# The recurrence's preparation of the first 256 tokens beside the projection's last 15 tiles

## The reference

```python
h = rms_norm(x, norm_w[l], 1e-6)
proj = h @ w_in[l]                        # 1024 -> 4224 columns, 33 blocks of 128
cols, gate, q, k, v, diff_gate = split(proj)   # cols: r | k | v | decay in | rate in
shifted = concat([prev_row, cols[:-1]])
r, k, v, xw, xa = split(cols + (shifted - cols) * shift_mu)
w = -softplus(-(decay_w0 + tanh(xw) @ decay_lora_b)) - 0.5
decay, a = exp(-exp(w)), sigmoid(iclr_a0 + xa @ iclr_lora_b)
kk = l2_normalised_per_head(k * key_k);  k = k * (1 + (a - 1) * key_a)
# per head, token after token:
S = S * decay + (S @ -kk) (kk * a)^T + v k^T;   y = S @ r
```

## Time and profile before

| what | value |
|---|---|
| median of 3 runs | 4490.38 us |
| the profiled execution's own time | 4491.03 us |
| its span, first to last instruction | 4489.1 us |
| mean granted TensorE clock | 0.949 |
| busy: PE, DVE, ACT, POOL | 4002.1, 2066.5, 1726.1, 519.2 us |
| projection matmuls, three lines together | 929.9 + 934.4 + 918.1 us |

### The profile page before, as it was taken

One profiled execution on the slowest core, in us unless ns is written; L12 is line 12 of the kernel. 1 busy time (PEld: TensorE's weight loads), 2 busy tenths in 40 slices (PEclk: granted clock), 3 DMA queues, 4 the chain that ended last, 5 costly groups with the idle time before them and its releaser, 6 DMA issues.

```text
span 4489.1 us, 113506 instructions
## 1 busy us (share of the span) xinstructions
PE 4002.1 (89%) x49138; PEld 3486.6 (78%) x49138; DVE 2066.5 (46%) x4539; ACT 1726.1 (38%) x3547; POOL 519.2 (12%) x273
## 2 busy tenths in 40 slices
PE   7999999699978888879899999988999698988798
PEld 7999999588865565558899999976888555655588
DVE  6111111678845555554331111117887455565465
ACT  3000000677755665552200000006777465665421
POOL 5222221000000000011032222200000000000111
PEclk9999999799998999989999999988999898998899
DMA  3111111211114354344211111111111242543532
GB/s 139 72 71 72 68 67 52 69 42 50 45 52 138 124 177 140 92 148 163 98 71 72 69 70 71 72 63 43 46 51 35 82 156 85 174 137 93 172 136 83
DMA packets 224389, 410.46 MB, mean 91 GB/s; under 512 B 32402, under 2 KB 132756, under 8 KB 210068
## 3 DMA queue, kind: packets, MB, share of 16 engines
q1 hardware_dynamic: 208916, 313.75, 22.2%
q10 hardware_dynamic: 14976, 89.46, 5.0%
HBM read 296.39 MB, written 106.76 MB: 90 GB/s over the span
## 4 chain that ended last, share of the span: by engine, by line
PE 68%; DVE 11%; ACT 10%; issue 5%; PEld 3%; DMA 2%; SPq 2%; POOL 0%; ACTq 0%; DVEq 0%; PEldq 0%
PE psum L2148 11%; PE psum L2145 11%; PE psum L2147 11%; PE psum L1374 4%; PE psum L1402 4%; PE psum L717 2%; PE psum L1390 2%; ACT arena L1178 2%; PE psum L1138 2%; PE psum L1708 2%; PE psum L1709 2%; PE psum L1710 2%; PE psum L788 1%; DVE arena L1294 1%; PE psum L1130 1%
## 5 line engine op out<-in xcount | busy, mean ns | idle before, releaser
L2145 PE MATMUL psum<-x_hi,w_parts 128*128 128x416 f32 x2640 | 929.9, 352 | 44.3 <-POOL w_parts L2066 18.4
L2148 PE MATMUL psum<-x_hi,w_parts 128*128 128x416 f32 x2640 | 934.4, 354 | 0.0
L2147 PE MATMUL psum<-x_lo,w_parts 128*128 128x416 f32 x2624 | 918.1, 350 | 0.0
L2078 DVE TENSOR_TENSOR arena<-psum,arena 128x416 f32<-128x416 f32 x330 | 195.2, 593 | 1240.4 <-PE psum L2148 1236.5
L334 ACT ACTIVATE arena<-arena 128x256 f32<-128x256 f32 x16 | 8.0, 501 | 1479.2 <-DVE arena L462 1479.2
L2145 PEld LDWEIGHTS psum<-x_hi,w_parts 128*128 128x128 f32 x2640 | 497.7, 189 | 51.4 <-POOL w_parts L2066 20.9
L2147 PEld LDWEIGHTS psum<-x_lo,w_parts 128*128 128x128 f32 x2624 | 494.5, 188 | 8.9 <-issue 0.6
L2148 PEld LDWEIGHTS psum<-x_hi,w_parts 128*128 128x128 f32 x2640 | 497.1, 188 | 3.1
L1281 DVE TENSOR_SCALAR_CACHE_REDUCE arena<-psum 128x512 f32<-128x512 f32 (+3 forms) x640 | 357.7, 608 | 295.3 <-PE psum L1374 158.7
L1402 PE MATMUL psum<-arena 128*128 128x128 f32 x2176 | 310.7, 285 | 64.0 <-ACT arena L1187 46.8
L1374 PE MATMUL psum<-arena 64*128 64x512 f32 (+3 forms) x1280 | 324.3, 610 | 39.7 <-DVE arena L1281 21.7
(11 more groups left out here) (348 smaller groups left out, 6650.5 us busy)
## 6 DMA issues: line engine op xcount, KB each, us to landing
out_proj_t<-arena ACTq DMA_DIRECT2D x66, 1040.5 KB, 4.2
arena<-in_cache_k SPq DMA_DIRECT2D x256, 256.0 KB, 2.9
arena<-in_cache_v SPq DMA_DIRECT2D x256, 256.0 KB, 3.0
arena<-in_w_in SPq DMA_DIRECT2D x66, 512.0 KB, 3.5
arena<-out_proj_t SPq DMA_DIRECT2D x96, 257.0 KB, 3.3
arena<-out_proj_t SPq DMA_DIRECT2D x24, 1024.0 KB, 5.9
x_res<-in_x SPq DMA_DIRECT2D x10, 1664.0 KB, 13.2
m_raw<-mixed_t SPq DMA_DIRECT2D x8, 1664.0 KB, 10.9
```

The costliest lines, as they stand in the source:

```text
L2078: dve.tensor_tensor(ost[:, b % 2, 1 + g * TG:1 + (g + 1) * TG], bank[q % banks_of(l)][:, 0:TG], RSTD[:, cols(g)], ALU.mult).then_inc(p_ev, 1)
L2145: pe.matmul(bank[q % n][:, 0:TG], w_hi[:, b % 3, k, :], x_hi[:, g, k, :], start=(k == 0), stop=False)
L2147: pe.matmul(bank[q % n][:, 0:TG], w_hi[:, b % 3, k, :], xl, start=False, stop=False)
L2148: mm = pe.matmul(bank[q % n][:, 0:TG], w_lo[:, b % 3, k, :], x_hi[:, g, k, :], start=False, stop=(k == KT - 1))
```

## The change

- The last three blocks are taken group by group rather than block by block. The order of the 15 tiles is (30,0), (31,0), (30,1), (32,0), (31,1), (32,1), then (30,2), (31,2), (32,2) and so on. `LEAD_TILE` is the index of the first.
- These 15 tiles are stored one by one by SyncE, each right after its eviction; blocks 0 to 29 are stored as before by ScalarE. Block 32's evictions wait for the stores of block 30's tiles in the same `ost` buffer. The end of the phase waits for the stores on SyncE.
- Slots -4 to -2 of the recurrence are issued in the projection: ScalarE's as `rwkv_scalar(act, LEAD)` behind its last store, VectorE's between evictions, TensorE's ten steps at the tile's start or half (`LEAD_STEPS`), SyncE's loads between the tile stores. The recurrence itself runs from slot -1, with the raw rows of m = 2 loaded in the projection too.
- Six constants are loaded behind the weights, the three masks after tile 5. VectorE waits for six (L457 waited for nine), and for the masks only in the recurrence.
- GpSimd's memset of a column of E moves to the end of its projection program.
- Bank 3 is kept for the preparation: both layers' tiles use seven banks, 0 to 2 and 4 to 7; layer 0's sums of squares go to bank 3 rather than 7.
- The recurrence's arrays are placed anew in SBUF. Those that the first 256 tokens need lie in x_lo's first two groups; `raw`, the copies and other working arrays of m = 0 and 1 in x_hi's first two groups and the raw weight buffers, so they may be written when the tiles of these groups (and the last weight split) are done.
- Semaphores that both phases use are no longer shared with other phases.

```diff
-        SLOTS = range(-4, NU + 3)
+        LEAD, SLOTS = range(-4, -1), range(-1, NU + 3)
...
+        def load_raw(sp, l, m):
+            if m:
+                pV.wait(sp, m - 1, sV_XV)
+            for j in (1, 0, 2):
+                in_raw.inc(sp.dma_start(raw[:, j, :, :], rows(l, j * RW + m % 2 * 2 * P, 2 * P, 2, m // 2 * TQ, TQ + 1)))
+            in_raw.close()
...
             for s in SLOTS:
                 u, t, n, q, r, m, lt = roles(s)
                 if lt is not None:
...
+                    load_lora(sp, l, lt)
+                if m is not None and m > 2:
+                    load_raw(sp, l, m)
...
-            for s in SLOTS:
+            for s in slots:
                 u, t, n, q, r, m, lt = roles(s)
                 if m is not None:
                     mixes(m)
+                if m == 0:
+                    act.wait_ge(p_mm, LEAD_TILE + 6)
+                    act.wait_ge(p_ws, CB + 1)
...
-        SEQ_P = [(b, g) for g in range(NG) for b in range(2)] + [(b, g) for b in range(2, CB) for g in range(NG)]
+        SEQ_P = [(b, g) for g in range(NG) for b in range(2)] + [(b, g) for b in range(2, CB - 3) for g in range(NG)]
+        LEAD_TILE = len(SEQ_P)
+        SEQ_P += [(CB - 3 + i, g) for i, g in ((0, 0), (1, 0), (0, 1), (2, 0), (1, 1), (2, 1))] + [(b, g) for g in range(2, NG) for b in range(CB - 3, CB)]
+        LEAD_STEPS = {(5, 1): (0, sT_ZW), (6, 1): (0, sT_ZA), (7, 1): (0, sT_SS), (8, 1): (0, sT_RN), (9, 0): (0, sT_BO),
+                      (10, 0): (1, sT_ZW), (10, 1): (1, sT_ZA), (11, 1): (1, sT_SS), (12, 0): (1, sT_RN), (13, 0): (1, sT_BO)}
...
-        banks_of = lambda l: 8 if l else 7
+        PB = (0, 1, 2, 4, 5, 6, 7)
...
         def proj_sync(sp, l):
...
+            lead_consts(sp, l)
+            sp.wait_ge(p_st[0], stores(l, 0) + 16 * 7)
+            sp.wait_ge(p_st[1], stores(l, 1) + 16 * 7)
+            load_lora(sp, l, 0)
+            for i, (b, g) in enumerate(SEQ_P[LEAD_TILE:]):
+                sp.wait_ge(p_ev, LEAD_TILE + i + 1)
+                c = slice(0 if g == 0 else 1 + g * TG, 1 + (g + 1) * TG)
+                sp.dma_start(PT[bass.ds(l * COLS + b * P, P), c], ost[:, b % 2, c]).then_inc(p_st[b % 2], 16)
+                if i == 3:
+                    load_raw(sp, l, 0)
+                if i == 5:
+                    lead_masks(sp)
+                if i == 7:
+                    load_raw(sp, l, 1)
+                    load_lora(sp, l, 1)
+                if i == 11:
+                    load_raw(sp, l, 2)
+            for u in range(2):
+                sp.wait_ge(p_st[u], stores(l + 1, u))
...
-            for b in range(CB):
+            for b in range(CB - 3):
                 act.wait_ge(p_ev, LAST[b] + 1)
                 act.dma_start(PT[bass.ds(l * COLS + b * P, P), :], ost[:, b % 2, :]).then_inc(p_st[b % 2], 16)
-            for u in range(2):
-                act.wait_ge(p_st[u], stores(l + 1, u))
+            rwkv_scalar(act, LEAD)
...
-            for q in range(2 * NG, len(SEQ_P)):
+            for q in range(2 * NG, LEAD_TILE):
                 evict(q)
+            lead_vector(dve)
+            for i in range(6):
+                evict(LEAD_TILE + i)
+            for m in range(2):
+                if m:
+                    prep_vector(dve, 0, sV_BV)
+                    pV.close()
+                else:
+                    dve.wait_ge(p_ws, CB + 1)
+                mixed_vector(dve, m, sV_XK)
+                mixed_vector(dve, m, sV_XR)
+                mixed_vector(dve, m, sV_XV)
+                if m:
+                    evict(LEAD_TILE + 9)
+                prep_vector(dve, m, sV_LD)
+                prep_vector(dve, m, sV_SCAN)
+                evict(LEAD_TILE + (10 if m else 6))
+                for k in (sV_KF, sV_RKB, sV_MX, sV_RC, sV_R, sV_K):
+                    prep_vector(dve, m, k)
+                if m:
+                    lora_vector(dve, 1)
+                evict(LEAD_TILE + (11 if m else 7))
+                for k in (sV_KKN, sV_A, sV_BB, sV_B):
+                    prep_vector(dve, m, k)
+                evict(LEAD_TILE + (12 if m else 8))
+            for i in (13, 14):
+                evict(LEAD_TILE + i)
...
                 for k in range(KT):
                     if q == 0 and k == 4:
                         pe.wait_ge(p_ws, 2)
+                    if k % 4 == 0 and (q - LEAD_TILE, k // 4) in LEAD_STEPS:
+                        m, step = LEAD_STEPS[q - LEAD_TILE, k // 4]
+                        if step == sT_ZW and m == 0:
+                            pe.wait_ge(r_cst, 16 * 6)
+                        prep_tensor(pe, m, step)
+                        if step == sT_BO:
+                            pT.close()
```

More of the change, by code:

```diff
@@ L2 @@
 import math
+from collections import namedtuple
 from contextlib import ExitStack
@@ L214, in build @@
         phase_sems()
[L215 to L218, removed]
+        x_group = KT * TG
+        x_hi_at = KT * TOK
+        RA0 = cv(4, 2, TQ)
+        Bf0, Kf0, Vf0, bv0 = [cv(4, TQ) for _ in range(4)]
+        mX1, mL, eye2 = cv(CH), cv(len(LEVELS), CH), cv(CH)
+        assert cv.at <= 2 * x_group
+        cv.at = 2 * x_group
+        RA1, RA2 = cv(4, 2, TQ), cv(4, 2, TQ)
+        Bf1, Kf1, Vf1, bv1, bv2 = [cv(4, TQ) for _ in range(5)]
+        Z = cv(3, 4, CH)
+        assert cv.at <= x_hi_at
+        cv.at = x_hi_at
+        raw = cv(3, 2, TQ + 1)
+        after_raw = cv.at
+        cop_first = cv(3, 2, TQ)
+        assert cv.at <= x_hi_at + x_group
+        cv.at = x_hi_at + x_group
+        xk_first, xr_first, tw_first, ta_first, L_first, kf_first = [cv(2, TQ) for _ in range(6)]
+        assert cv.at <= x_hi_at + 2 * x_group
+        cv.at = 2 * KT * TOK + 6 * KT * P
+        kkn_first, rkb_first, Ei_first = [cv(2, TQ) for _ in range(3)]
+        assert cv.at <= 2 * KT * TOK + 8 * KT * P
+        cv.at = after_raw
         BS, SK = cv(3, 8, 3, CH), cv(3, 8, 2, CH)
@@ L451, in rwkv_scalar, with mixed_vector @@
                     lora_tanh(lt)
-        def rwkv_gpsimd(pool, l):
-            pool.memset(E[:, :, :, 0:1], 1.0).then_inc(r_once, 1)
-        def rwkv_vector(dve, l):
-            dve.wait_ge(r_cst, 16 * 9)
-            dve.memset(Z[:, :, :, :], 0.0)
+        def mixed_vector(dve, m, k):
+            j, dst = {sV_XK: (1, prep_of(m).xk), sV_XR: (0, prep_of(m).xr), sV_XV: (2, Vf[m // 2 % 2][:, m % 2 * 2:m % 2 * 2 + 2, :])}[k]
+            pA.wait(dve, m, {sV_XK: sA_CK, sV_XR: sA_CR, sV_XV: sA_CV}[k])
+            for c in range(2):
+                i_ = dve.scalar_tensor_tensor(dst[:, c, :], raw[:, j, c, 0:TQ], prm[:, m % 2 * 2 + c, j:j + 1], prep_of(m).cop[:, j, c, :], ALU.mult, ALU.add)
+            pV.inc(i_)
@@ L515, in lora, with rwkv_vector @@
[L515 to L520 removed]
+            lora_vector(dve, 0)
+        def rwkv_vector(dve, l):
+            dve.wait_ge(r_msk, 16 * 3)
+            dve.memset(Z[:, :, :, :], 0.0)
             def masked(u, v):
@@ L2069, in proj_gpsimd @@
                         low(pool, g, p_lp, True)
+            pool.memset(E[:, :, :, 0:1], 1.0).then_inc(r_once, 1)
         def proj_vector(dve, l):
@@ L2073, in evict @@
                 b, g = SEQ_P[q]
-                if b >= 2:
+                if b == CB - 1:
+                    sent = sum(x[0] % 2 == b % 2 for x in SEQ_P[LEAD_TILE:q])
+                    dve.wait_ge(p_st[b % 2], stores(l, b % 2) + 16 * ((CB - 3) // 2 + sent))
+                elif b >= 2:
                     dve.wait_ge(p_st[b % 2], stores(l, b % 2) + 16 * (b // 2))
```

314 lines of the change are left out of this document (159 added, 155 removed).

## The result

The changed kernel took 4417.9 us (median of 4 runs, 4411.85 to 4421.63), the kernel before 4490.91 (4 runs, 4482.67 to 4492.69). The ratio is 0.9842 [0.9823, 0.9862]: faster by 73 us, where 64 were forecast. The profiled execution took 4421.63, its span is 4419.8.

What follows compares the result with a forecast made beforehand. TensorE alone bounds the last 15 tiles, then 48.5 us a layer lie on the path; after the change 11.5 + 3.5 + 1.5 = 16.5. Gain 64.0 for two layers: 4491.0 - 64.0 = 4427.0 us, own range 4414 to 4438.

Steps and rivals of the forecast that it cites:

- Term 1: TensorE's ten preparation steps inside the last 15 projection tiles, paid in full: 11.5 us a layer, ends 10.5 and 14.
- The waits: In the 15 tiles every TensorE step has its input in time: 0 us, four steps with 1.2 to 1.5 to spare.
- Term 2: From the last store's issue to the first scores: 3.5 us with the smaller store, ends 3.3 and 5.2.
- Term 3: Slot -1 starts at a slow granted clock: +1.5 us a layer, ends +3 and -3.6.
- rival D: Over the hand-over the clock never falls, since 4.3 us idle is close to 3.5: 4417 us; chance 0.05.
- A: Steps in the 15 tiles wait some 1.5 us at four margins: 4439 us, up to 4450 with clock falls; chance 0.16.
- B: Waits in the 15 tiles let the clock fall and it stays down: slower, 4560 us; chance 0.04.
- C: Something else holds the recurrence's start, half or less of 32 us a layer gained: 4459 to 4490; chance 0.05.
- much over 19 us: Sign of being wrong: slot -1, the recurrence's first slot behind the barrier, lasting much longer than 19 us.
- Other stages changed by more than 2 us: Sign of being wrong: attention or output projection, outside the changed stretch, differing by more than 2 us.
- L723 5 to 6 us behind the last projection matmul: Expected profile sign at the hand-over: first scores starts 5 to 6 us after the last projection matmul, some 32 us earlier.

Runs made afterwards that it cites:

- warm_slot_again: Changed kernel plus 12 unread projection matmuls over the hand-over and 19 small ones in slot -1; 4424.84 us, against 4427.26 for the changed kernel beside it.

## Why the prediction was right

**What bounds it.** TensorE alone set the 15 tiles, and all between the last store and `scores` was on the path: the profile after bears out both, since the tiles grew by TensorE's own steps alone (79.13 of 79.13 us busy) while VectorE took on 24.5 us and ScalarE 22.8 at no cost.

**Term 1, the ten steps:** 11.5 forecast, 11.13 measured in each layer. The 1.23 us that the warm weight loads gave for the four-instruction steps already held the change between two kinds of matmul; the doubling showed the mean step to be 0.86 of matmuls and 0.26 paid once. The upper end of 14 added 0.25 a step for this a second time. That the 0.26 is this change is a reading and not isolated by a run.

**The waits:** none forecast, none seen. The clock that the prediction set up tile by tile, against layer 0 of the profile after (0 at 715.27; "ready" is the end of the instruction that makes the input):

| step | stands, forecast | stands | ready, forecast | ready | margin |
|---|---|---|---|---|---|
| ZA, m = 0 | 30.6 | 30.7 | 29.2 | 29.4 | 1.3 |
| SS, m = 0 | 36.2 | 36.4 | 33.5 | 33.5 | 2.9 |
| RN, m = 0 | 41.9 | 41.9 | near 38 | 38.0 | 3.9 |
| BO, m = 0 | 45.2 | 45.3 | 44.0 | 44.0 | 1.4 |
| ZA, m = 1 | 54.2 | 54.4 | 52.9 | 52.9 | 1.5 |
| SS, m = 1 | 59.8 | 60.1 | 57.0 | 57.2 | 2.9 |
| RN, m = 1 | 63.1 | 63.4 | 61.6 | 61.7 | 1.7 |
| BO, m = 1 | 68.7 | 69.0 | 65.2 | 65.4 | 3.7 |

No entry is off by more than 0.35 us. This table is the part of the forecast that could have turned it: with the steps half a tile to one and a half tiles earlier, and VectorE's order as it was, 28 us are lost.

**Term 2, the hand-over:** 3.5 forecast from issue to L768, 3.16 in layer 0. The small store landed in 2.1 us rather than 2.5; the barrier behind it takes the 1.0 that 0.8 and 0.2 had assumed. In layer 1 the hand-over is 0.36 us longer (4.14 against 3.78). The Trainium skill (DMA: Bandwidth & Descriptors, Anatomy of one DMA) gave an estimate of 2.5 for this store by its fixed part and its rate, in a section on transfers that GpSimd issues, while this store is issued by SyncE; the trace has 2.1, so page and row differ and the row decides. By the page's rate of 436 GB/s the 208 KB take an estimated 0.5, which leaves some 1.6 us fixed instead of 2.0.

**Term 3, the clock:** +1.5 forecast for slot -1, +1.83 and +1.67 measured. The fall came 2.8 us after the last matmul instead of 3.5 (0.86 mean over 3.93 us, 0.50 after), which with an idle stretch of 3.93 us disposes of rival D. The size was right, the way there was not, so that the size came out is luck: +1.5 stood for two or three slow blocks before the clock returned, and +3 for a slot that stays slow up to where it is slow already. The second is what the trace shows, 0.50 without a break from 798.33 to 817, and it cost 1.8. What a full clock in the slot is worth can be read from warm_slot_again: 16.76 and 16.75 us against 20.95 and 21.10, 4.2 and 4.4 with the added matmuls in it, where the prediction had 5.1 between its +1.5 and its -3.6.

**The sum:** 11.13 + 3.16 + 1.83 = 16.1 us in layer 0 against 16.5 forecast, so a gain of 32.4 against 32.0, and 64.6 for two layers against 64.0. The profiled spans differ by 69.3, of which 4.7 lie in the rest of the program (4216.7 against 4212.0 in the last table), and the medians by 73.0. As the rest differs by up to 16 us between profiles without any edit, the 9 us over the forecast are within chance. Timed side by side three times, the medians differ by 73.0, 61.2 and 54.1; all 12 runs of the changed kernel have a mean of 4423.7 and the 21 of the kernel before beside them 4486.1, which is 62.5 apart.

**The rivals.** A was refuted for this kernel; waits of its size, from another source, were shown for steps that stand earlier. B did not occur. C fell with 3.16 us from store to `scores`. D fell with the granted clock of 0.86 over the hand-over and 0.50 behind it.

**The signs of being wrong.** Two of the list came true without the forecast being wrong. A slot -1 "much over 19 us" was there, 20.9, but the forecast's own +1.5 already put it at 20.6. Other stages changed by more than 2 us, which is no sign, since the kernel before differs from itself by 10.3 us in one of them. The list also puts L723 5 to 6 us behind the last projection matmul, while the working has 4.3; it was 3.93.

## What to carry to other kernels

A sparse preparation can be laid beside a stretch that one engine fills, and then costs only that engine's own instructions, here 0.86 us of matmuls and 0.26 paid once at each of ten steps, against 48.5 us of hand-over, loads and engines that waited for each other in turn. Whether it holds is decided by a table of when each step stands and when its input is ready; write it down tile by tile from the durations in the trace. Put the other engines' evictions in the same table, since moving the steps alone by half a tile to one and a half tiles lost 28 us of the gain, most of it in waits that VectorE's fixed order made. And measure both kernels more than once before a difference of 10 us is explained: here it was chance in a stage that the change doesn't touch.

## What was not expected of the hardware

- The clock did not come back under full load: from 798.33 to 808.00 TensorE is busy 9.67 of 9.67 us, mostly with matmuls on 64 rows, and the granted clock stays at 0.50 (1.2 GHz), and so on past 817 (6.70 of 9.00 us busy from 808.00). In the kernel before it returned at 836.10, after the run from 832.03. With 12 projection matmuls over the hand-over and 19 matmuls of 128x128 by 128 columns in the slot the clock stays at 1.00 for all 16.8 us. What made the difference between these was not isolated.
- In the kernel with the steps earlier, the same waits of 1.0 to 2.7 us, 11.2 in all, left the clock at 1.00 in layer 0 and brought it down three times for some 3.3 us each in layer 1.
- A step of four to sixteen small matmuls between the projection's costs 0.86 us for its matmuls and 0.26 once, and doubling its matmuls does not double the 0.26. That the 0.26 is the change between two kinds of matmul was not isolated.
